# Half of the dense gates by indirect adds into a zeroed DRAM matrix: a hybrid retention, sparse-attention and PEER layer on one core

## The reference, cut to what matters

```python
q = (xt @ wq).reshape(n, PEER_HEADS, 2, PEER_DQ // 2)
s = jnp.einsum('nhpd,pkd->nhpk', q, subkeys)
sv, si = lax.top_k(s, PEER_TOPK)
cand = sv[:, :, 0, :, None] + sv[:, :, 1, None, :]
...
gate = jax.nn.softmax(cs.astype(jnp.float32), axis=-1).astype(x.dtype)
...
hid = jax.nn.gelu(jnp.einsum('cd,chkd->chk', xc, u[ec]))
return jnp.einsum('chk,chkd->cd', gc * hid, v[ec])
```

## Time and profile before

| | us |
|---|---|
| median of 3 runs | 1794.88 (1794.35 to 1795.64) |
| span of the profiled execution | 1793.2 |
| TensorE busy | 1774.3, 99% |
| VectorE busy | 1388.5, 77% |
| ScalarE busy | 766.7, 43% |
| POOL busy | 170.8, 10% |
| HBM traffic over the span | 294 GB/s |

### The profile page before, as it was taken

The page is one execution under the profiler, slowest core; times in us unless marked ns, Lnnn a source line. Parts: engine busy times, 40 slices in busy tenths (PEclk is TensorE's granted clock), DMA queues, the critical chain, the costliest instruction groups (busy, mean ns, idle before and its releaser), DMA issues.

```text
span 1793.2 us, 27943 instructions
## 1 busy us (share of the span) xinstructions
PE 1774.3 (99%) x10680; PEld 1591.7 (89%) x10680; DVE 1388.5 (77%) x2153; ACT 766.7 (43%) x1054; POOL 170.8 (10%) x158
## 2 busy tenths in 40 slices
PE   8999999999999999999999999999999999999998
PEld 8899989789999999999977777789999998777775
DVE  6546667566459796888378898989999998898996
ACT  5334444655331010111155555555555555555555
POOL 0000000000000121222100000111111111111010
PEclk9999999999999999999999999999999999999999
DMA  9774544556545987998999899999999999999984
GB/s 351 262 280 149 165 141 142 188 187 226 187 150 192 358 333 282 342 336 331 362 377 361 317 324 341 344 350 367 377 369 374 377 347 361 353 359 365 357 309 152
DMA packets 77275, 531.01 MB, mean 296 GB/s; under 512 B 8811, under 2 KB 9211, under 8 KB 16268
## 3 DMA queue, kind: packets, MB, share of 16 engines
q1 hardware_dynamic: 54512, 377.96, 56.6%
q0 software_dynamic: 22352, 151.59, 23.2%
q10 hardware_dynamic: 332, 0.44, 0.1%
HBM read 512.60 MB, written 15.20 MB: 294 GB/s over the span
## 4 chain that ended last, share of the span: by engine, by line
PE 97%; DVE 1%; issue 1%; ACT 1%; DMA 0%; DVEq 0%; SPq 0%; ACTq 0%
PE bank L918 19%; PE bank L934 11%; PE bank L596 8%; PE bank L597 8%; PE bank L598 8%; PE bank L1015 6%; PE bank L1014 6%; PE bank L1019 6%; PE bank L1021 6%; PE bank L1020 6%; PE bank L935 5%; PE bank L973 2%; PE bank L743 0%; PE bank L952 0%; PE bank L791 0%
## 5 line engine op out<-in xcount | busy, mean ns | idle before, releaser
L1932 DVE TENSOR_TENSOR lo<-raw,hi 128x1024 fp32r<-128x1024 f32 x384 | 463.6, 1221 | 101.7 <-ACT hi L1318 101.3
L1318 ACT ACTIVATE hi<-raw 128x1024 fp32r<-128x1024 f32 x384 | 404.9, 1059 | 320.8 <-PE bank L1021 233.5
L918 PE MATMUL bank<-hT,raw 128*128 128x192 f32 x2048 | 337.4, 326 | 0.0
L918 PEld LDWEIGHTS bank<-hT,raw 128*128 128x128 f32 x2048 | 332.3, 190 | 0.1
L934 PE MATMUL bank<-xr,hi 128*128 128x384 f32 x1024 | 291.3, 359 | 0.0
L935 PE MATMUL bank<-xr,lo 128*128 128x192 f32 x1024 | 256.3, 250 | 0.0
L1444 DVE TENSOR_TENSOR lo<-raw,hi 128x2048 fp32r<-128x2048 f32 x75 | 171.8, 2290 | 103.7 <-ACT hi L1086 68.2
L1015 PE MATMUL bank<-lo,wm 128*64 128x512 f32 x512 | 202.8, 396 | 0.0
L1014 PE MATMUL bank<-hi,wm 128*128 128x512 f32 x512 | 199.9, 390 | 1.7 <-DVE wm L1987 1.2
L1019 PE MATMUL bank<-lo,wm 128*128 128x512 f32 x512 | 200.3, 391 | 0.0
L1021 PE MATMUL bank<-hi,wm 128*128 128x512 f32 x512 | 199.3, 389 | 0.0
(11 more groups left out here) (293 smaller groups left out, 2686.2 us busy)
## 6 DMA issues: line engine op xcount, KB each, us to landing
raw<-in_u SPq DMA_DIRECT2D x128, 1024.0 KB, 7.7
raw<-in_v SPq DMA_DIRECT2D x128, 1024.0 KB, 7.2
raw<-in_w_in SPq DMA_DIRECT2D x43, 1024.0 KB, 5.8
raw<-in_w_out SPq DMA_DIRECT2D x16, 1024.0 KB, 4.8
raw<-in_wq SPq DMA_DIRECT2D x16, 1024.0 KB, 4.8
gate_matrix<-gs POOLq DMA_DIRECT2D x12, 768.0 KB, 12.5
gs<-gate_matrix SPq DMA_DIRECT2D x12, 768.0 KB, 9.2
raw<-in_cmp_w SPq DMA_DIRECT2D x8, 1024.0 KB, 4.8
```

The source lines that it names most:

```text
L918: last = mm(bank[s % 2][:, 0:TD], raw[:, s, k * P:(k + 1) * P], xn[:, k, 0:TD], start=(k == 0), stop=(k == KT - 1))
L1318: do(hi[:, s % 2, cols], raw[:, s, cols], ACT.Copy).then_inc(v_hi_ready, 1)
L1932: vec.tensor_tensor(lo[:, n % 2, cols], raw[:, n % RAW, cols], hi[:, n % 2, cols].bitcast(F32), ALU.subtract).then_inc(v_lo_ready, 1)
```

## The change

64 tokens of each tile of 128 keep the one-hot products: MATRIX_T is 64 to 127. The other 128 dense tokens (0 to 63 and 128 to 191) get their gates another way:

- POOL writes zeros over the whole `gate_matrix`, which now holds all 16 groups of experts, in eight transfers during the projection (`clear`).
- VectorE computes the cell of each choice in that matrix (`find_cells`), after each route_tokens.
- POOL moves the cells and the gates to 128 partitions (`move_cells`), and adds each gate to its cell with an indirect transfer that accumulates (`add_gate`), 128 cells at a time. There are 64 of these for each tt. Heads can choose the same cell, so before each group of eight POOL waits until all earlier ones have landed. Those of tt=1 are laid over blocks 14 to 29, those of tt=0 over blocks 32 to 53, and stand ahead of the block's fetches.
- In the first v stage VectorE now multiplies gates from DRAM into `hidden` for the first 32 blocks too, for the 128 tokens; SP loads the first two groups ahead of v block 4, once all adds and stores have landed.
- The gelus of the sparse pairs in the u stage are placed five blocks later (GELU_LAG).

```diff
-GATE_BLOCKS, BATCHES = HALF - ROUTED, TD // 8
+MATRIX_T = range(64, P)
+GATE_BLOCKS, BATCHES = HALF - ROUTED, len(MATRIX_T) // 8
...
+ADDED = SLOTS // 2
+ADD_WINDOWS = {1: (14, 30), 0: (32, 54)}
+ZERO_PARTS, ZERO_W = 8, 2 * TD
+GELU_LAG = 5
...
+def added_by(tt, b):
+
+    first, last = ADD_WINDOWS.get(tt, (0, 0))
+    return ADDED * min(max(b + 1 - first, 0), last - first) // (last - first) if last else 0
...
 def gelus_at(b):
 
-    return [q for q in range(PAIR_TILES // GROUP) if items_by(b - 1) >= group_end(q) > items_by(b - 2)]
+    def seen(b):
+        return items_by(b - 1 - (GELU_LAG if b < HALF else 0))
+
+    return [q for q in range(PAIR_TILES // GROUP) if seen(b) >= group_end(q) > seen(b - 1)]
...
+                if half == 0:
+                    for r in range(RAW):
+                        load_v(r, r)
+                    sp.wait_ge(gates_added, 16 * ADDED * 2)
+                    for x in range(2):
+                        sp.wait_ge(gate_stored[x], 16 * (BATCHES // 4))
+                    for g in range(2):
+                        load_gates(g, g)
...
+            def clear(c):
+
+                pool.wait_ge(block_done, PAIRS + 4 * (c + 1))
+                n = TD * NKEYS // ZERO_PARTS
+                pool.dma_start(gate_parts[:, c * n:(c + 1) * n].rearrange("p (a w) -> p a w", w=ZERO_W),
+                               zeros.unsqueeze(1).to_broadcast([P, n // ZERO_W, ZERO_W])).then_inc(gate_zeroed, 16)
...
+            def move_cells(tt):
+
+                gates = choice[:, 2, tt]
+                pool.wait_ge(choices_listed, {1: 2, 0: 3}[tt])
+                for src, dst in ((cells[:, tt, :], cell_at), (gates, cell_gate)):
+                    by_head = src.rearrange("p (h x k) -> p x h k", h=PH, x=2)
+                    for x in range(2):
+                        pool.dma_start(dst[TS * x:TS * (x + 1), tt, :].rearrange("p (h k) -> p h k", h=PH),
+                                       by_head[0:TS, x]).then_inc(choices_moved, 16)
...
+            def add_gate(tt, n):
+
+                h, k = n // (PK // 2), n % (PK // 2)
+                if n == 0:
+                    pool.wait_ge(choices_moved, {1: 96, 0: 160}[tt])
+                    pool.wait_ge(gate_zeroed, 16 * ZERO_PARTS)
+                elif k == 0:
+                    pool.wait_ge(gates_added, 16 * (n + {1: 0, 0: ADDED}[tt]))
+                pool.indirect_dma_start(gate_cells, bass.IndirectOffsetOnAxis(ap=cell_at[:, tt, n:n + 1], axis=0),
+                                        cell_gate[:, tt, n:n + 1], None, compute_op=ALU.add).then_inc(gates_added, 16)
...
+                for tt in (1, 0):
+                    for n in range(added_by(tt, b - 1), added_by(tt, b)):
+                        add_gate(tt, n)
                 ahead = range(items_by(b - 1), items_by(b))
...
-            for x in range(6):
-                last = nc.tensor.transpose(bank[2 + x // 4][:, (x % 4) * P:(x % 4 + 1) * P], choice[:, x // 2, x % 2, :], ident)
+            for x in range(3):
+                last = nc.tensor.transpose(bank[2][:, x * P:(x + 1) * P], choice[:, x, 0, :], ident)
...
+            def find_cells(tt):
+
+                f, u = cells_f, cells[:, tt, :]
+                step(vec.tensor_copy(u, choice[:, 1, tt]))
...
+                vec.tensor_copy(u, f).then_inc(choices_listed, 1)
...
             dv.wait_ge(choices_ready, 1)
+            find_cells(1)
...
             route_tokens(0, FIRST_GATHERS)
+            dv.wait_ge(choices_ready, 2)
+            find_cells(0)
             items_to(FIRST_GATHERS)
...
+                    if half == 0 and mv < GATED_EARLY:
+                        rest = gated_rows.rearrange("p (a t) -> p a t", t=TS)[:, 0:3:2, :]
+                        gates_of = gates_of.rearrange("p (a t) -> p a t", t=TS)[:, 0:3:2, :]
+                        vec.tensor_tensor(rest, rest, gates_of, ALU.mult).then_inc(gated, 1)
```

More of the change, by code:

```diff
@@ L480, in load_gates @@
                     sp.dma_start(gs[:, g, 0:TD * GROUP_J], gate_dram[q].rearrange("i t j -> i (t j)")).then_inc(gate_loaded[g], 16)
[L482 to L492, removed]
+                if half == 0:
[6 more added lines that the diff above has]
+                        load_gates(g, g)
+                for q in range(HALF // GROUP_J):
                     if half and q == 3:
@@ L495, in _ @@
                         sp.dma_start(h_first, res_dram[:, 0:1024]).then_inc(gf_loaded, 16)
-                    x = first + q - early
+                    x = HALF // GROUP_J * half + q
                     if x >= 2:
@@ L500, in _ @@
                     for r in range(GROUP_J):
-                        load_v(GROUP_J * q + r, r % RAW)
+                        if half or q or r >= RAW:
+                            load_v(GROUP_J * q + r, r % RAW)
             sp.wait_ge(block_done, m_v(1) + 8)
@@ L533, in _ @@
                 pool.dma_start(bias[:, :, P * part:P * part + P * (part + 1)], skew).then_inc(bias_loaded, 16)
+            pool.wait_ge(consts_ready, 2)
+            def clear(c):
[3 more added lines that the diff above has]
+                               zeros.unsqueeze(1).to_broadcast([P, n // ZERO_W, ZERO_W])).then_inc(gate_zeroed, 16)
+            for c in range(ZERO_PARTS // 2):
+                clear(c)
             pool.wait_ge(acc_evacuated, RK + 4)
@@ L539, in _ @@
                                ).then_inc(halves_swapped, 16)
+            for c in range(ZERO_PARTS // 2, ZERO_PARTS):
+                clear(c)
             pool.wait_ge(acc_evacuated, M_WQ)
@@ L1344, in round_gated @@
                 weights = hidden[:, mv * TD:(mv + 1) * TD]
+                ac.wait_ge(gated, mv + (HALF * half + 1))
                 if half or mv >= GATED_EARLY:
-                    ac.wait_ge(gated, mv + (HALF * half + 1) - GATED_EARLY)
                     weights = wmt[:, (mv % 2) * TD:(mv % 2 + 1) * TD]
@@ L1370, in _ @@
                     for part in range(3):
-                        do(choiceT[:, part, :], bank[2 + part // 2][:, (part % 2) * T:(part % 2 + 1) * T], ACT.Copy).then_inc(ch_copied, 1)
+                        do(turned[:, part, :], bank[2][:, part * P:(part + 1) * P], ACT.Copy).then_inc(ch_copied, 1)
                 if ROUTED + 2 <= r < ROUTED + 2 + BATCHES:
@@ L1385, in _ @@
                         round_split(2 * HALF * half + mv)
-                        if half and mv < 2:
-                            hidden_gelu(HALF - 2 + mv)
-                        round_gated(half, mv)
+                    if half and mv < 2:
+                        hidden_gelu(HALF - 2 + mv)
+                    round_gated(half, mv)
                     pair_gelus((2 * half + 1) * HALF + mv)
@@ L1885, in route_tokens @@
                 vec.tensor_tensor(gates, gates, small[:, 0:PH].unsqueeze(2).to_broadcast([P, PH, PK]), ALU.mult).then_inc(choices_ready, 1)
+            step(vec.scalar_tensor_tensor(out=cells_f, in0=ident, scalar=float(GROUP_J), in1=iota, op0=ALU.mult, op1=ALU.mult,
+                                          accum_out=token_at[:, 0:1]))
+            routed()
+            step(vec.tensor_scalar(token_at[:, 1:2], token_at[:, 0:1], float(GROUP_J * P), None, ALU.add))
+            routed()
             route_tokens(1, 0)
             dv.wait_ge(choices_ready, 1)
+            find_cells(1)
             step(vec.tensor_copy(picked[:, 1], choice[:, 2, 1]))
```

78 lines of the change are left out of this document (52 added, 26 removed).

## The result

The changed kernel takes 1926.96 us (median of 4 runs, 1923.66 to 1931.09) against 1794.88: the ratio is 1.0738, 95% interval 1.0723 to 1.0754. It is slower by 132 us, and the range of the prediction ended at 1838. The profiled execution has a span of 1923.6 us, 130.4 more than before.

The account below looks back on a forecast made before the run. TensorE, busy 99% of the span, was taken as the bound. 1793.2 - 28.8 + 29.1 + 12.2 + 4.4 + 0.5 = 1810.6; the runs' median lies 1.7 higher: 1812 us, range 1800 to 1838.

Parts of the forecast that it names:

- The forecast case: At block 32 of the u stage TensorE waits 20 to 55 us for the choices; chance 0.45.
- Length of POOL's run: U stage: 75 indirect transfers at 1.3 us, 97.5 us, before item 11's fetch leaves at 699.2; TensorE then waits 29.1 us.
- The bound above (2.74): Upper price of one add on POOL, 2.44 + 0.30 us, with which TensorE's wait at block 32 would be 120 us.
- They end in time: Blocks 32 on: the tt=0 adds and POOL's other work, some 130 us, fit into 175 and cost nothing.
- First v block: Start of the first v stage: TensorE waits for the late gate load, +12.2 us, 11 to 16 by the landing's ends.
- Clock: After two TensorE waits of over 10 us the slow pace returns, 2.2 us each: +4.4 us, bounds 0 and 4.4.
- Zeroing: The first of eight zero writes may hold up a weight tile in the compression stage: 0 to 4 us, 0.5 taken.
- The tail behind item 11's fetch: Landing and VectorE's work on items 11 to 13 take 19.6 us, so the choices are there at 718.8.
- the 28.8 us that leave TensorE: One-hot batches fall from 24 to 8 (28.5 us) and transposes from six to three (0.33): -28.8 us.
- the multiplies of the first 32 v blocks: VectorE's 32 extra multiplies in mv 0 to 31, 13 us on 118 of 146, cost nothing.
- item 7's gelu: U stage: item 7's dot comes at about 670, before block 29 ends, so ScalarE does not stand on the gelu.
- The rival with adds bound by their landing: Landing, not issue, bounds the adds: wait of 90 us at block 32, 1873 us or more; chance 0.13.

Follow-up runs that it names:

- plain_writes: The changed kernel with its 128 adds as plain indirect writes of the same words, without accumulation: 1864.04 us, ratio 1.0378.
- tt0_adds: The changed kernel with only the 64 adds of rows tt=0 (blocks 32 to 53), the other tile's left out: 1844.12 us, ratio 1.0258.
- no_adds: The changed kernel without its 128 adds; zeroing, find_cells, move_cells and the late gate load stay: 1790.59 us, ratio 0.9974.
- before_zeroing: The kernel before the change plus the eight 1.5 MB clears, into a matrix that nothing reads: 1798.76 us, ratio 1.0023.
- exp_31: The changed kernel with ScalarE's exponentials of the second choices at block 31 in place of 27: 1928.54 us, ratio 1.0750.
- tt1_adds: The changed kernel with only the 64 adds of rows tt=1 (blocks 14 to 29), the second tile's left out: 1875.29 us, ratio 1.0451.
- half_rows: The changed kernel with each of the 128 adds cut to 64 of its 128 partitions: 1909.47 us, ratio 1.0629.
- one_tile: The changed kernel with 64 adds (tt=1, blocks 14 to 59), 16 batches of products, first two gate groups loaded behind v tile 1: 1824.24 us.

## Why the prediction was wrong

The forecast case named the right mechanism, POOL's adds ahead of the fetches on which the choices wait, and the side was right. The time was not. The profile's 1923.6 us against the sum's 1810.6 are 113.0 us, and these terms, measured less predicted, make 112:

- **Length of POOL's run, 49.6 us.** This is the step that failed first. An indirect transfer was priced at 1.3 us by the fetch; an add costs 1.55 + 0.30, and 1.71 + 0.30 in the mean. Item 11's fetch left at 755.3 instead of 699.2, and the last tile's choices, predicted at 718.8, came at 774.0. TensorE lost 42.5 + 36.2 = 78.7 us where 29.1 stood; that is 5.7 less than the 55.2 us by which the choices were late, since TensorE came later itself, after the zeroing and with slow products. The bound above (2.74) held the price; the value chosen was that of the nearest row, and no row had an accumulation in it. plain_writes shows the same row to hold for a plain write, in the median. A part of 7.1 us is the start: first add at 600.4 instead of 593.3. The list came at 589.0 (586.3 by the sum), and the two landings ahead of the adds were waited for 4.1 and 3.3 us where 1.5 and 1.9 stood.
- **"They end in time", 44.0 us.** The tt=0 adds were priced at nothing because 130 us of POOL's work fit into 175. The gate batches wait 15.3 us and the pair gelus 28.7. tt0_adds shows 54 us for these adds alone. They needed 200 us; and that they end in time was the wrong question, for each fetch between them has a time of its own by which it must leave. The prediction named this place only as what would make it wrong.
- **First v block, 7.9 us.** 20.05 instead of 12.2. The 12.2 were right where the gates come last (no_adds), in part by luck: the terms as written add up to 11.9, and the landing took 8.3 us instead of the 8 assumed. Here the last gathers come later still, a path that the prediction did not have.
- **Clock, 7.5 us.** The products after each long wait begin at the 1.2 GHz pace: 13.46 us for 64 that take 10.57 undisturbed, 12.12 for the next 64, 5.93 and 3.75 for 5.37 and 1.95, 18.87 for 15.76, and ten products of the first v block at 0.43 instead of 0.23. That is 11.9 us for five gaps, against 4.4. The size for one gap, 2.2, was right (2.0 in no_adds after 12.2 us); there were more gaps, and some cost 2.4 to 3.1. The granted clock reads 0.6 in two slices that hold the first two gaps. The Trainium skill's "TensorE: Matmul & The Clock Gate" (Part 1) has the half rate as the default that sustained work lifts; the trace agrees after each of the five gaps.
- **Zeroing, 3.3 us.** 3.8 in the span of before_zeroing where 0.5 stood, within the bounds; 3.2 of it are one wait in the stage named.

The tail behind item 11's fetch has a slip of its own: its terms add up to 19.45 and not 19.6, which changes nothing here.

What held: the 28.8 us that leave TensorE (the sum for no_adds closes within 1 us with them), the first v block by itself, one clock loss, that the multiplies of the first 32 v blocks cost nothing, and that item 7's gelu holds nobody. ScalarE stood at the exponentials instead, a wait not named, which moved 42 us of the debt forward and added none (exp_31).

The rival with adds bound by their landing got the size nearly right (90 us at block 32) for a reason that the trace does not bear out: in tt1_adds the waits for landings are 7.4 us for all 64, of some 150 from the first to the last. For the tt=0 adds it was partly right, 40.8 of 200 us. The Trainium skill's "DMA: Bandwidth & Descriptors" (Specifications), which has small transfers done as read-modify-write, spoke for that rival. Plain writes of 4 bytes took no longer on POOL than fetches of whole rows, so on POOL the size of the words is not what costs. What it does to the landings no run here separates from the accumulation.

Two things stay open: why an accumulating transfer holds POOL longer than a plain one, and why some indirect transfers take 2.2 to 3.5 us on POOL in place of their usual time. The latter are there before, too.

## What to carry to other kernels

A queue that idles between waits is not free: price an instruction put into it against each wait behind it, not against the stage's total. Here 64 adds, two behind each fetch, made TensorE wait 6.6 us for the choices, and 0.5 once the list of pairs went ahead of the cells (and less was zeroed and loaded); one or two adds ahead of each block's fetches made it wait 21.5. And when a stage gets shorter, ask which chain of gathers was just as long as it: 13 us won in the u stage brought nothing until three gathers were moved out of it.

## What the runs showed of the hardware

- In the median, an indirect transfer with accumulation to DRAM holds POOL 1.55 us with 128 single words (after), 1.41 with 64 (half_rows); the same as a plain indirect write 0.96 (plain_writes). A gather of 128 rows mostly takes 0.94 to 1.0. About 0.30 us lie before the next in each case.
- The accumulating form left 144 packets under 512 B in the queue for 128 words, 80 for 64; the plain form 32 for 128.
- The means are 0.15 to 0.33 us above the medians (1.71 against 1.55, and 1.91 against 1.58 in one_tile, where one or two adds stand between fetches), so a chain is priced by the mean.
- A short wait of TensorE can bring the slow clock back, too: behind 2.1 us in no_adds the granted clock reads 0.60 to 0.67 up to 869.5, and 96 instructions take 1.8 us longer.
